# Gates of a decoder's first 128 tokens by indexed adds in a DRAM table in place of one-hot products

## The chip, the cores and the metric

One NeuronCore of a Trainium2 chip runs the whole program in one launch. The metric is device microseconds of one execution; three executions of the kernel before gave 2060.58, 2060.9 and 2061.28 us, and their median, 2060.9 us, is the time before. Its engines are called by the profile's names: PE (TensorE, matmul), PEld (its weight loads), DVE (VectorE), ACT (ScalarE), POOL (GpSimd) and SP (SyncE, which here only issues DMAs).

## What is computed

Two layers, each a mixer (gated convolution beside an mLSTM), a cross-attention on a memory, and a feed-forward part of 16,384 single-neuron experts, on 256 tokens of width 1024. The change is in the last part:

```
q  = (xb @ w_pq).reshape(tokens, 8 heads, 2, 128)
sc = einsum('thpc,hpkc->thpk', q, sub_keys)        # two score lists of 128 keys per head
sv, si = top_k(sc, 16)
cand = sv[..., 0, :, None] + sv[..., 1, None, :]   # 256 sums
fv, fi = top_k(cand, 16)
eid = row key * 128 + column key                   # of each of the 16
g   = softmax(fv)
a   = gelu(ue[eid] . xb)
out = sum over heads and k of g * a * ve[eid]
```

The kernel does not gather experts. It computes the Gelu of all 16,384 for all tokens, multiplies by a dense table of gates, gate[column key, row key, token], which is zero for what was not chosen, and multiplies with all of v_experts. What has to be made is that table: per token 8 heads x 16 weights, added at (row, column).

## The kernel before, in words

All weights pass as 680 slabs of 128 x 1024 floats (512 KB), 340 a layer, through four slots. SP loads raw[j]; ACT copies it to w_hi[j] (in rounded form); DVE subtracts, w_lo[j] = raw[j] - w_hi[j] (`lo_part`, line 848); PE takes the products hi x (hi, lo) as one matmul of 512 columns (line 1345) and lo x hi as one of 256 (line 1346), eight such chunks a slab. A slot is free again when PE is done with it, so DVE can be up to four slabs ahead of PE, and SP's loads four ahead of DVE.

In each layer the experts' first side (U) has 128 slabs, the second (V) 128. In U slab n PE makes 128 x 256 sums; ACT copies one half (`half_of`, line 721) and splits the slab n + 4 (line 725), DVE adds the other half (`add_u`, line 1113), ACT takes the Gelu (`gelu_of`, line 731), and SP stores the 128 KB of h_out in DRAM (h_park). h_out has two slots, so `half_of` waits for the store of two slabs before. In V, SP loads those back (h_in), POOL multiplies each by gate[:, n, :] (`gated`, line 524), ACT and DVE split the product, and PE multiplies it with the slab (line 1733).

While PE works through U slabs 4 to 71, DVE also makes the choice, as a written-out list of instructions. `top16` (lines 1126 to 1138) takes the 16 largest of two rows at a time, for 32 score lists and 16 candidate lists (one block of 128 tokens on the partitions after the other). Then come the decoding of the places into keys (lines 1172 to 1206, with 2 x 16 picks of 256 elements and two trees), ACT's Exp of all weights at U slab 60 (`EXP_AT`, line 753), and their normalising (lines 1211 to 1213, `decoded`). Between these, `spend(us)` adds up an assumed cost and emits `next_lo()` (one `add_u` and one `lo_part`) for each 1.56 us of it (`LO_EVERY`), so the order on DVE is fixed when the program is built. Steps that depend on the one before are joined by a semaphore (`step.join`, `step.link`).

At U slab 70 (`RET_AT`) PE waits for `decoded` and transposes the rows, columns and weights of both token blocks (line 1697, six transposes), so that tokens lie on the free axis. From slab 72 (`HOT_AT`) to 123, 64 groups of four tokens follow: DVE builds one-hots (`hot_rows`, lines 1228 to 1242, four operations of 512 elements), PE multiplies column one-hots by weighted row one-hots, 4 tokens x 2 parts a group (`gates_of`, line 1708), and ACT copies the 128 x 512 result into the gate table (`gate_out`, line 761). GROUP_AT places the groups between PE's chunks, in pairs, one pair every 13 chunks.

POOL's queue in a layer, in order: a load of memT, sums of squares (line 494), scaling of z, sums of squares of the x after the mixer; then the wait for the slab XO_AT and the load of the keys skT (line 507), the sums of squares before the queries, whose result PE needs for the norm (x_mean_square), scaling of the queries; then a wait for the last one-hot and the load of par (line 516); then the 128 multiplies of V. During U it has nothing to do.

Of the kernel before, what the change touches and what calls it, by code (L numbers as in the profile page):

```python
# [22 lines left out]
FP32 = mybir.dt.float32  # L23
# [9 lines left out]
P = 128  # L33
# [66 lines left out]
GROUPS = T // 4  # L100
HOT_AT = 72
RET_AT = 70
EXP_AT = 60
# [5 lines left out]
GROUP_AT = tuple(FIRST_PAIR + (n - n % 2) * HOT_SLABS * KB // GROUPS for n in range(GROUPS))  # L109
EARLY = RING - 1  # L110
# [39 lines left out]
def trunk(nc, x, mem, slabs, params, sub_keys, out):  # L150
    ctx = ExitStack()
    with ctx:
# [50 lines left out]
        pick_at = at("pick_at", top[0], [P, 2, T // 2, 2], FP16)  # L203
        g_parts = at("g_parts", top[0] + 2 * T * 2, [P, T // 2, PARTS, 2], FP16)
        top[0] += (2 + PARTS) * T * 2
        top[0] = (top[0] + LINE - 1) // LINE * LINE
        gated_at = top[0]
        gate = sb("gate", [P, NKEYS, T])
# [78 lines left out]

        h_park = nc.dram_tensor("h_park", (NKEYS, P, T), FP32, kind="Internal").ap()
# [48 lines left out]
        settled = sem("settled")  # L337
        act_step, dve_step, out_ready = sem("act_step"), sem("dve_step"), sem("out_ready")
# [119 lines left out]
        def _(pool):  # L458
# [11 lines left out]

            def scale(dst, count, evacs, xns):
# [25 lines left out]
            for layer in range(DEPTH):  # L497
# [7 lines left out]
                sum_chunks(layer, SUM_OUT, 0)  # L505
                pool.wait_ge(slab_done, layer * SLABS + XO_AT)
# [11 lines left out]
                settle(pool)  # L518

                def gated(g, j, h, n):  # L520
# [3 lines left out]
                    nc.gpsimd.tensor_tensor(h[:, n:n + 1, :], h[:, n:n + 1, :], gate[:, ds(g * RING + j, 1), :],  # L524
                                            ALU.mult).then_inc(gated_ready, 1)
# [16 lines left out]
        def _(act):  # L542
# [73 lines left out]
            for layer in range(DEPTH):  # L616
# [142 lines left out]
                def gate_out(n):  # L759
                    act.wait_ge(gate_mm, layer * GROUPS + n + 2)  # L760
                    nc.scalar.activation(gate[:, :, 4 * n:4 * n + 4],  # L761
                                         ps[:, 4 + n % RING, :].rearrange("p (t i) -> p i t", t=4),
                                         ACT.Copy, scale=1.0 / GATE_SCALE).then_inc(gate_copied, 1)
# [78 lines left out]
        def _(dve):  # L842
# [119 lines left out]
            for layer in range(DEPTH):  # L962
# [179 lines left out]
                for n in range(0, TB * SETS, 2):  # L1142
                    if n % SETS == 0:
                        dve.wait_ge(sc_evac, layer * TB + n // SETS + 1)
                        settle(dve)
                    src = (scores0, scores1)[n // SETS]
                    step.join()
                    top16(*[(src[:, m % SETS, :], struck[:, m - n, 0:NKEYS], top_v[:, m, :], top_u[:, m, :])
                            for m in (n, n + 1)], us=0.29)
                step.join()  # L1150
                step.mark(nc.vector.tensor_copy(top_i[:], top_u[:]))

                step.join()
                for b in range(TB):
                    tops = top_v[:, b * SETS:(b + 1) * SETS, :].rearrange("p (h s) a -> p h s a", s=2)
                    step.join()
                    first = 0
                    for a0, na, nb in CAND:
                        shape = [P, PH, na, nb]
                        step.mark(nc.vector.tensor_tensor(  # L1160
                            cand[:, :, first:first + na * nb].rearrange("p h (a b) -> p h a b", a=na),
                            tops[:, :, 0, a0:a0 + na].unsqueeze(3).to_broadcast(shape),
                            tops[:, :, 1, 0:nb].unsqueeze(2).to_broadcast(shape), ALU.add))
                        first += na * nb
                    spend(1.3)
                    for n in range(b * PH, (b + 1) * PH, 2):
# [3 lines left out]
                step.join()  # L1170

                nc.vector.tensor_tensor(g_exp[:], fin_v[:], fin_v[:, :, 0:1].to_broadcast([P, TB * PH, TOPK]),
                                        ALU.subtract).then_inc(fin_ready, 1)
                flat_i = fin_i[:].rearrange("p c k -> p (c k)")
                step.mark(nc.vector.tensor_scalar(bit_u[:], flat_i, 8, None, ALU.bitwise_and))
                step.mark(nc.vector.tensor_scalar(low_u[:], flat_i, 7, None, ALU.bitwise_and))
                step.mark(nc.vector.tensor_scalar(by16_u[:], flat_i, 4, None, ALU.logical_shift_right))
                step.mark(nc.vector.tensor_scalar(by8_u[:], flat_i, 3, None, ALU.logical_shift_right))
                step.mark(nc.vector.tensor_copy(at_f[:], flat_i))
                spend(1.6)  # L1180
                step.join()


                step.mark(nc.vector.scalar_tensor_tensor(bit_f[:], at_f[:], float(CAND[0][1] * CAND[0][2]), bit_u[:],
                                                         ALU.is_lt, ALU.mult))
                step.mark(nc.vector.scalar_tensor_tensor(b_f[:], at_f[:], float(N_CAND - CAND[2][1]), low_u[:],
                                                         ALU.is_lt, ALU.mult))
                step.mark(nc.vector.scalar_tensor_tensor(a_f[:], by8_u[:], -2.0, by16_u[:], ALU.add, ALU.max))
                step.join()
                step.mark(nc.vector.tensor_tensor(b_at[:], b_f[:], bit_f[:], ALU.add))  # L1190
                step.mark(nc.vector.scalar_tensor_tensor(a_at[:], at_f[:], float(CAND[2][0] - (N_CAND - CAND[2][1])), a_f[:],
                                                         ALU.add, ALU.max))
                spend(2.2)
                keys = top_i[:].rearrange("p (c s) a -> p c s a", s=2)
                for side, (place, found) in enumerate(((a_at, row_f), (b_at, col_f))):
                    step.join()
                    for a in range(TOPK):
                        step.mark(nc.vector.scalar_tensor_tensor(  # L1198
                            pick[:, a], place[:].rearrange("p (c k) -> p c k", k=TOPK), float(a),
                            keys[:, :, side, a].unsqueeze(2).to_broadcast([P, TB * PH, TOPK]), ALU.is_equal, ALU.mult))  # L1200
                        spend(0.45)
                    n = TOPK // 2
                    while n:
                        step.join()
                        out = found[:].rearrange("p (o c k) -> p o c k", o=1, k=TOPK) if n == 1 else pick[:, 0:n]
                        step.mark(nc.vector.tensor_tensor(out, pick[:, 0:n], pick[:, n:2 * n], ALU.add))
                        spend(0.13 * n + 0.2)
                        n //= 2
                step.join()
                dve.wait_ge(gexp_ready, layer + 1)  # L1210
                step.link(nc.vector.tensor_reduce(g_sum[:], g_exp[:], AX.X, ALU.add))
                step.link(nc.vector.reciprocal(g_sum[:], g_sum[:]))
                nc.vector.scalar_tensor_tensor(g_exp[:], g_exp[:], GATE_SCALE,
                                               g_sum[:].unsqueeze(2).to_broadcast([P, TB * PH, TOPK]),
                                               ALU.mult, ALU.mult).then_inc(decoded, 1)
# [3 lines left out]
                step.mark(nc.vector.tensor_copy(pick_at[:].rearrange("p i n e -> p (i n e)"), ps[:, 4, :]))  # L1219
                g_pairs = ps[:, 5, 0:T].rearrange("p (n e) -> p n e", e=2)  # L1220
# [111 lines left out]
        def _(pe):  # L1332
# [94 lines left out]
            for layer in range(DEPTH):  # L1427
# [267 lines left out]
                for i, src in enumerate((row_f[:], col_f[:], g_exp[:].rearrange("p c k -> p (c k)"))):  # L1695
                    for b in range(TB):
                        last = nc.tensor.transpose(ps[:, 4 + i // 2, (i % 2) * T + b * P:(i % 2) * T + (b + 1) * P],
                                                   src[:, b * P:(b + 1) * P], ident[:])
# [117 lines left out]
```

## Time and profile before

| | |
|---|---|
| median of three executions | 2060.9 us (2060.58 to 2061.28) |
| the profiled execution's own time | 2061.37 us |
| its span, first to last instruction | 2059.6 us |
| PE, PEld busy | 99%, 85% |
| DVE, ACT, POOL busy | 80%, 58%, 16% |
| granted TensorE clock, mean | 0.999 |
| DMA, mean over the span | 211 GB/s |

The profile shows one execution. Busy shares are averages over stages with different limits; the windows give them by stage. An instruction's row says when it began, how long it lasted and, in brackets, how long its engine had been idle and what ended that; instructions of one engine are pipelined, so the distance between two starts can be shorter than a duration. In layer 0 the choice runs from about 288 us, the gate groups from 493 to 665 us, and V from 678 us.

### The profile page before, as it was taken

How to read it: one execution, taken by the hardware profiler on the slowest of the kernel's cores; microseconds unless marked ns; L12 is line 12 of the kernel's file. 1: busy time of each engine (PE TensorE's matmuls, PEld its weight loads, DVE VectorE, ACT ScalarE, POOL GpSimd, SP SyncE). 2: the span in 40 equal slices, each digit the busy share in tenths (PEclk: the TensorE clock that was granted, in tenths of full speed). 3: DMA queues.
4: the chain of work that ended last, by engine and by line, in shares of the span. 5: the costliest groups of instructions: out<-in, count | busy, mean ns of one | idle time of the engine just before them, and what ended most of it. 6: DMA issues, size and time to landing. Idle time of an engine off the chain costs nothing.

```text
span 2059.6 us, 38391 instructions
## 1 busy us (share of the span) xinstructions
PE 2042.0 (99%) x11552; PEld 1756.4 (85%) x11552; DVE 1643.4 (80%) x3047; ACT 1190.0 (58%) x1901; POOL 337.0 (16%) x342
## 2 busy tenths in 40 slices
PE   8999999999999999999999999999999999999998
PEld 7888888888888888888888888888888898888886
DVE  7785869999998667767688858799999986776666
ACT  6655556667666555555565545666666665545553
POOL 3010110000000333335330102000000004333331
PEclk9999999999999999999999999999999999999999
DMA  6445456776555877777654555566665567777773
GB/s 232 148 154 175 172 193 237 236 233 216 196 199 196 265 241 241 262 241 242 211 188 135 186 170 169 195 237 236 223 215 197 200 215 255 240 241 262 242 241 124
DMA packets 174249, 435.54 MB, mean 211 GB/s; under 512 B 19504, under 2 KB 85040, under 8 KB 173136
## 3 DMA queue, kind: packets, MB, share of 16 engines
q1 hardware_dynamic: 173520, 430.06, 62.2%
q0 software_dynamic: 640, 4.32, 0.6%
q8 instruction: 53, 0.87, 0.2%
q14 instruction: 36, 0.29, 0.1%
HBM read 397.60 MB, written 36.70 MB: 211 GB/s over the span
## 4 chain that ended last, share of the span: by engine, by line
PE 93%; DVE 4%; ACT 1%; DMA 1%; issue 1%; SPq 0%; DVEq 0%; ACTq 0%
PE ps L1733 33%; PE ps L1345 32%; PE ps L1346 16%; PE ps L1708 3%; PE ps L1624 2%; PE ps L1339 2%; DVE w_lo L848 1%; DMA raw<-slabs 1%; PE ps L1755 1%; PE ps L1683 1%; PE ps L1649 1%; PE ps L1606 1%; ACT w_hi L725 0%; DMA h_park<-h_out 0%; DVE pick L1198 0%
## 5 line engine op out<-in xcount | busy, mean ns | idle before, releaser
L848 DVE TENSOR_TENSOR w_lo<-raw,w_hi 128x1024 fp32r<-128x1024 f32 x674 | 838.2, 1244 | 265.9 <-ACT w_hi L793 195.4
L1345 PE MATMUL ps<-act,w_hi 128*128 128x512 f32 x2784 | 986.0, 397 | 0.0
L1346 PE MATMUL ps<-act,w_lo 128*128 128x256 f32 x2784 | 776.4, 279 | 0.0
L1345 PEld LDWEIGHTS ps<-act,w_hi 128*128 128x128 f32 x2784 | 521.9, 187 | 115.2 <-issue 0.4
L1733 PE MATMUL ps<-w_hi,act 128*128 128x512 f32 x1936 | 596.4, 389 | 0.0
L1346 PEld LDWEIGHTS ps<-act,w_lo 128*128 128x128 f32 x2784 | 525.0, 189 | 0.3
L793 ACT ACTIVATE w_hi<-raw 128x1024 fp32r<-128x1024 f32 x248 | 263.1, 1061 | 326.8 <-PE ps L1733 326.8
L1733 PEld LDWEIGHTS ps<-w_hi,act 128*128 128x128 f32 x1936 | 363.4, 188 | 75.7
L1733 PE MATMUL ps<-w_lo,act 128*128 128x512 f32 x968 | 376.6, 389 | 0.0
L524 POOL TENSOR_TENSOR h_in<-h_in,gate 128x256 f32<-128x256 f32 x250 | 243.6, 976 | 437.5 <-DMA h_in<-h_park 437.5
L725 ACT ACTIVATE w_hi<-raw 128x1024 fp32r<-128x1024 f32 x248 | 261.1, 1053 | 0.0
L1733 PEld LDWEIGHTS ps<-w_lo,act 128*128 128x128 f32 x968 | 181.7, 188 | 37.5
L552 ACT ACTIVATE w_hi<-raw 128x1024 fp32r<-128x1024 f32 x168 | 177.1, 1054 | 47.9 <-PE ps L1346 26.6
L1264 DVE TENSOR_TENSOR act<-h_in,act 128x256 fp32r<-128x256 f32 x250 | 184.5, 738 | 4.9 <-ACT act L781 4.9
L731 ACT ACTIVATE h_out<-h_out 128x256 f32<-128x256 f32 x248 | 103.2, 416 | 124.6 <-DVE h_out L1113 122.8
L721 ACT ACTIVATE h_out<-ps 128x256 f32<-128x256 f32 x248 | 94.6, 382 | 120.5 <-PE ps L1346 106.8
L516 POOL DMA_DIRECT2D par<-params x2 | 1.2, 592 | 785.7 <-DVE hot_row L1242 785.7
L1113 DVE TENSOR_TENSOR h_out<-h_out,ps 128x256 f32<-128x256 f32 x248 | 102.1, 412 | 16.3 <-ACT h_out L721 16.0
L781 ACT ACTIVATE act<-h_in 128x256 fp32r<-128x256 f32 x250 | 100.0, 400 | 8.3 <-POOL h_in L524 8.3
L1242 DVE TENSOR_TENSOR hot_row<-row_is,g_parts 128x512 f16<-128x512 f16 x256 | 96.5, 418 | 0.0
L1345 PE MATMUL ps<-pre,w_hi 128*128 128x512 f32 x216 | 77.1, 400 | 0.0
L761 ACT ACTIVATE gate<-ps 128x512 f32<-128x512 f32 x128 | 70.4, 591 | 6.0 <-PE ps L1708 6.0
(268 smaller groups left out, 1818.3 us busy)
## 6 DMA issues: line engine op xcount, KB each, us to landing
raw<-slabs SPq DMA_DIRECT2D x680, 512.0 KB, 4.2
h_park<-h_out SPq DMA_DIRECT2D x256, 128.0 KB, 2.1
h_in<-h_park SPq DMA_DIRECT2D x250, 128.0 KB, 3.9
memT<-mem POOLq DMA_DIRECT2D x2, 1024.0 KB, 7.9
skT<-sub_keys POOLq DMA_DIRECT2D x2, 1024.0 KB, 6.3
x_park<-xT SPq DMA_DIRECT2D x2, 1024.0 KB, 6.4
xT<-x_park SPq DMA_DIRECT2D x2, 1024.0 KB, 7.3
xT<-x SPq DMA_DIRECT2D x4, 256.0 KB, 5.7
```

The costliest lines, as they stand in the source:

```text
L524: nc.gpsimd.tensor_tensor(h[:, n:n + 1, :], h[:, n:n + 1, :], gate[:, ds(g * RING + j, 1), :], ALU.mult).then_inc(gated_ready, 1)
L552: nc.scalar.activation(w_hi[:, j].rearrange("p k c -> p (k c)"), raw[:, j, :], ACT.Copy).then_inc(hi_ready, 1)
L725: nc.scalar.activation(w_hi[:, j].rearrange("p k c -> p (k c)"), raw[:, j, :], ACT.Copy).then_inc(hi_ready, 1)
L731: nc.scalar.activation(slot, slot, ACT.Gelu).then_inc(act_evac, 1)
L781: nc.scalar.activation(hi[:, j:j + 1, :], h[:, j:j + 1, :], ACT.Copy).then_inc(ga_hi_ready, 1)
L793: nc.scalar.activation(w_hi[:, j].rearrange("p k c -> p (k c)"), raw[:, j, :], ACT.Copy).then_inc(hi_ready, 1)
L848: nc.vector.tensor_tensor(w_lo[:, j].rearrange("p k c -> p (k c)"), raw[:, j, :], w_hi[:, j].rearrange("p k c -> p (k c)").bitcast(FP32), ...
L1113: nc.vector.tensor_tensor(slot, slot, ps[:, n % RING:n % RING + 1, 0:T], ALU.add).then_inc(u_sum, 1)
L1264: nc.vector.tensor_tensor(lo[:, j:j + 1, :], h[:, j:j + 1, :], hi[:, j:j + 1, :].bitcast(FP32), ALU.subtract).then_inc(ga_ready, 1)
L1345: nc.tensor.matmul(ps[:, j, :], w_hi[:, j, k, :], a[:, :, k, :], start=(k == 0), stop=False)
L1346: return nc.tensor.matmul(ps[:, j, hi * T:hi * T + T], w_lo[:, j, k, :], a[:, hi, k, :], start=False, stop=(k == KB - 1))
L1733: last = nc.tensor.matmul(ps[:, 2 * b + half, :], a[:, j, b * P:(b + 1) * P], w[:, j, 4 * half:4 * half + 4, :].rearrange("p k c -> p (k c)"),
```

## The change

The gates of tokens 0 to 127 are no longer made by one-hot products. A DRAM table g_spread of 128 x 128 x 128 floats (column key, row key, token) is zeroed by POOL during the query projections (eight stores of 1 MB, each awaited). For these tokens DVE computes an index, (column x 128 + row) x 128 + token, and the normalised weight; POOL then issues, per head, 16 indirect DMAs that add 128 weights (one per partition) at 128 indices each, and waits for a head's 16 before it goes on. When all eight heads are in, four loads of 2 MB bring the table into the first half of the gate tile, gate[:, 0]. Tokens 128 to 255 keep the one-hots, with 32 groups instead of 64, into gate[:, 1].

The choice is cut in three parts, (block 0, heads 0 and 1), (block 0, heads 2 to 7) and (block 1, all heads), each with its own top-16 steps, decoding, Exp and weights. A part's weights come after the first pair of the next part. ACT's Exps come at U slabs 12, 36 and 72; RET_AT moves from 70 to 78, HOT_AT from 72 to 80. PE transposes three matrices instead of six. The spend() figures are scaled to the parts' widths.

```diff
-GROUPS = T // 4
-HOT_AT = 72
-RET_AT = 70
-EXP_AT = 60
+GROUPS = P // 4
+HOT_AT = 80
+RET_AT = 78
+CHOICES = ((0, 0, 2), (0, 2, PH), (1, 0, PH))
+EXP_ATS = (12, 36, 72)
+ZERO_ROWS = 16
+BACK_ROWS = 32
...
-        gate = sb("gate", [P, NKEYS, T])
+        gate = sb("gate", [P, TB, NKEYS, P])
...
+        g_spread = nc.dram_tensor("g_spread", (P * NKEYS * P, 1), FP32, kind="Internal").ap()
...
 (POOL)
+            spread = g_spread.rearrange("(p n t) o -> p n (t o)", p=P, n=NKEYS)
...
                 sum_chunks(layer, SUM_OUT, 0)
+                nc.gpsimd.memset(zeros[:], 0.0).then_inc(zeros_set, 1)
+                pool.wait_ge(zeros_set, layer + 1)
+                for i in range(NKEYS // ZERO_ROWS):
+                    pool.dma_start(spread[:, i * ZERO_ROWS:(i + 1) * ZERO_ROWS, :], zeros[:]).then_inc(zeroed, 16)
+                    pool.wait_ge(zeroed, layer * (NKEYS // ZERO_ROWS * 16) + (i + 1) * 16)
                 pool.wait_ge(slab_done, layer * SLABS + XO_AT)
                 pool.dma_start(skT[:], ...)
...
+                for h in range(PH):
+                    for p in range(2):
+                        if h == CHOICES[p][1]:
+                            pool.wait_ge(place_ready, layer * 4 + 2 * p + 2)
+                    for i in range(h * TOPK, (h + 1) * TOPK):
+                        nc.gpsimd.indirect_dma_start(g_spread, bass.IndirectOffsetOnAxis(ap=place_u[:, i:i + 1], axis=0),
+                                                     g_flat[:, i:i + 1], None, compute_op=ALU.add).then_inc(scattered, 16)
+                    pool.wait_ge(scattered, (layer * PH + h + 1) * (TOPK * 16))
+                for n in range(0, NKEYS, BACK_ROWS):
+                    pool.dma_start(gate[:, 0, n:n + BACK_ROWS, :], spread[:, n:n + BACK_ROWS, :]).then_inc(spread_back, 16)
                 pool.wait_ge(hot_row_ready, (layer + 1) * GROUPS + 1)
...
+                pool.wait_ge(spread_back, (layer + 1) * (NKEYS // BACK_ROWS * 16))
...
 (ACT)
-                experts(RING, EXP_AT - RING)
-                act.wait_ge(fin_ready, layer + 1)
-                nc.scalar.activation(g_exp[:], g_exp[:], ACT.Exp).then_inc(gexp_ready, 1)
-                experts(EXP_AT, HOT_AT - RING - EXP_AT)
+                at = RING
+                for p, (b, h0, h1) in enumerate(CHOICES):
+                    exp_at = EXP_ATS[p]
+                    experts(at, exp_at - at)
+                    act.wait_ge(fin_ready, layer * len(CHOICES) + p + 1)
+                    chosen = g_exp[:, b * PH + h0:b * PH + h1, :]
+                    nc.scalar.activation(chosen, chosen, ACT.Exp).then_inc(gexp_ready, 1)
+                    at = exp_at
+                experts(at, HOT_AT - RING - at)
...
 (DVE)
+                def weights(p):
+                    b, h0, h1 = CHOICES[p]
...
+                    if b == 0:
+                        step.mark(nc.vector.scalar_tensor_tensor(place_f[:, own], col_f[:, flat], float(NKEYS), row_f[:, flat],
+                                                                 ALU.mult, ALU.add))
+                    dve.wait_ge(gexp_ready, layer * len(CHOICES) + p + 1)
+                    step.link(nc.vector.tensor_reduce(g_sum[:, cs], g_exp[:, cs], AX.X, ALU.add))
+                    step.link(nc.vector.reciprocal(g_sum[:, cs], g_sum[:, cs]))
+                    if b == 0:
+                        nc.vector.tensor_scalar(place_u[:, own], place_f[:, own], float(P), tok[:, 0:1],
+                                                ALU.mult, ALU.add).then_inc(place_ready, 1)
+                        nc.vector.tensor_tensor(g_flat[:, own]..., g_exp[:, cs], of_sum, ALU.mult).then_inc(place_ready, 1)
+                    else:
+                        nc.vector.scalar_tensor_tensor(g_exp[:, cs], g_exp[:, cs], GATE_SCALE, of_sum,
+                                                       ALU.mult, ALU.mult).then_inc(decoded, 1)
+                for p, (b, h0, h1) in enumerate(CHOICES):
+                    heads = h1 - h0
+                    wide = heads / PH
+                    for n in range(b * SETS + 2 * h0, b * SETS + 2 * h1, 2):
+                        step.join()
+                        top16(...)
+                        if p > 0 and n == b * SETS + 2 * h0:
+                            step.join()
+                            weights(p - 1)
+                            spend(0.9)
...
+                weights(len(CHOICES) - 1)
...
 (PE)
-                    for b in range(TB):
-                        last = nc.tensor.transpose(ps[:, 4 + i // 2, ...], src[:, b * P:(b + 1) * P], ident[:])
+                    last = nc.tensor.transpose(ps[:, 4, i * P:(i + 1) * P], src[:, P:2 * P], ident[:])
```

## Rows read from the trace of the kernel before

**Rows 1.** The page, part 1: busy us (share of the span) and instructions of each engine.

```profile
PE 2042.0 (99%) x11552; PEld 1756.4 (85%) x11552; DVE 1643.4 (80%) x3047; ACT 1190.0 (58%) x1901; POOL 337.0 (16%) x342
```

**Rows 2.** Windows: stretch, its us, busy us of each engine, clock, DMA share, GB/s.

```profile
140.00:235.00 95.00, 95.00 (x514) 82.46 (x514) 65.14 (x84) 49.15 (x80) 5.99 (x7) 1.00 0.49 166
...
320.00:484.00 164.00, 164.00 (x949) 144.61 (x948) 155.63 (x488) 106.52 (x180) 0.00 (x0) 1.00 0.69 231
```

**Rows 3.** Chain that ended last: start us, us, what; first and last of the gate pairs.

```profile
484.16 0.66 PE ps L1697 x6
...
504.23 0.98 PE ps L1708 x16
...
663.77 0.93 PE ps L1708 x16
```

**Rows 4.** Timeline of ACT around layer 1's Exp: start us, us, instruction, shapes.

```profile
1478.40 1.28 ACT L753 ACT_TABLE_LOAD   x1
...
1481.43 0.38 ACT L721 ACTIVATE h_out<-ps 128x256 f32<-128x256 f32 x1
1481.71 1.05 ACT L725 ACTIVATE w_hi<-raw 128x1024 fp32r<-128x1024 f32 x1
1482.78 1.28 ACT L731 ACT_TABLE_LOAD   x1
1484.07 0.42 ACT L731 ACTIVATE h_out<-h_out 128x256 f32<-128x256 f32 x1
```

**Rows 5.** DVE's waits, 440 to 492 us: us in total, times, longest.

```profile
DVE h_out L1113 <- ACT h_out L721: 1.9, 2, 1.5
DVE w_lo L848 <- ACT w_hi L725: 1.8, 4, 0.5
```

**Rows 6.** Windows of line 1345 alone (one matmul a chunk), PE and PEld busy.

```profile
310.00:470.00 160.00, 160.00 (x463) 86.25 (x462) 1.00 0.69 231
```

**Rows 7.** Timeline of DVE at the end of layer 0's choice.

```profile
480.75 1.22 DVE L848 TENSOR_TENSOR w_lo<-raw,w_hi 128x1024 fp32r<-128x1024 f32 x1
481.89 0.41 DVE L1211 TENSOR_REDUCE g_sum<-g_exp 128x16 f32<-128x256 f32 x1
482.33 0.25 DVE L1212 RECIPROCAL g_sum<-g_sum 128x16 f32<-128x16 f32 x1
482.62 0.42 DVE L1213 SCALAR_TENSOR_TENSOR g_exp<-g_exp,g_sum 128x256 f32<-128x256 f32 x1
482.96 0.41 DVE L1113 TENSOR_TENSOR h_out<-h_out,ps 128x256 f32<-128x256 f32 x1
```

**Rows 8.** Timeline of POOL, 120 to 300 us.

```profile
207.82 0.59 POOL L507 DMA_DIRECT2D skT<-sub_keys  x1 [65.58 <-PE ps L1624]
223.07 0.80 POOL L494 TENSOR_TENSOR sq_sum<-sq 128x256 f32<-128x256 f32 x1 [14.65 <-ACT sq L588]
```

**Rows 9.** DMA issues: engine, count, KB each, median us from issue to landing.

```profile
h_park<-h_out SPq DMA_DIRECT2D x256, 128.0 KB, 2.1
...
x_park<-xT SPq DMA_DIRECT2D x2, 1024.0 KB, 6.4
xT<-x_park SPq DMA_DIRECT2D x2, 1024.0 KB, 7.3
...
par<-params POOLq DMA_DIRECT2D x2, 62.0 KB, 3.1
```

**Rows 10.** POOL by line and operation: busy us, mean ns of one, idle before.

```profile
L516 POOL DMA_DIRECT2D par<-params x2 | 1.2, 592 | 785.7 <-DVE hot_row L1242 785.7
```

**Rows 11.** Timeline of POOL, 640 to 672 us.

```profile
663.11 0.59 POOL L516 DMA_DIRECT2D par<-params  x1 [392.93 <-DVE hot_row L1242]
669.54 3.42 POOL L524 TENSOR_TENSOR early_in<-early_in,gate 128x256 f32<-128x256 f32 x3 [5.84 <-DMA early_in<-h_park]
```

**Rows 12.** The page, part 5: a DVE subtract that runs beside POOL's multiplies.

```profile
L1264 DVE TENSOR_TENSOR act<-h_in,act 128x256 fp32r<-128x256 f32 x250 | 184.5, 738 | 4.9 <-ACT act L781 4.9
```

**Rows 13.** Timeline of DVE at the load of par.

```profile
662.38 1.22 DVE L848 TENSOR_TENSOR w_lo<-raw,w_hi 128x1024 fp32r<-128x1024 f32 x1
```

More of the change, by code:

```diff
@@ L760, in gate_out @@
                     act.wait_ge(gate_mm, layer * GROUPS + n + 2)
-                    nc.scalar.activation(gate[:, :, 4 * n:4 * n + 4],
+                    nc.scalar.activation(gate[:, 1, :, 4 * n:4 * n + 4],
                                          ps[:, 4 + n % RING, :].rearrange("p (t i) -> p i t", t=4),
@@ new lines, in _ @@
+                for p, (b, h0, h1) in enumerate(CHOICES):
+                    src = (scores0, scores1)[b]
+                    if h0 == 0:
+                        dve.wait_ge(sc_evac, layer * TB + b + 1)
+                        settle(dve)
+                    heads = h1 - h0
+                    wide = heads / PH
+                    for n in range(b * SETS + 2 * h0, b * SETS + 2 * h1, 2):
+                        step.join()
+                        top16(*[(src[:, m % SETS, :], struck[:, m - n, 0:NKEYS], top_v[:, m, :], top_u[:, m, :])
+                                for m in (n, n + 1)], us=0.29)
+                        if p > 0 and n == b * SETS + 2 * h0:
+                            step.join()
+                            weights(p - 1)
+                            spend(0.9)
+                    step.join()
+                    sets = slice(b * SETS + 2 * h0, b * SETS + 2 * h1)
+                    step.mark(nc.vector.tensor_copy(top_i[:, sets, :], top_u[:, sets, :]))
+                    tops = top_v[:, sets, :].rearrange("p (h s) a -> p h s a", s=2)
@@ L1158, in _ @@
                     for a0, na, nb in CAND:
-                        shape = [P, PH, na, nb]
+                        shape = [P, heads, na, nb]
                         step.mark(nc.vector.tensor_tensor(
-                            cand[:, :, first:first + na * nb].rearrange("p h (a b) -> p h a b", a=na),
+                            cand[:, h0:h1, first:first + na * nb].rearrange("p h (a b) -> p h a b", a=na),
                             tops[:, :, 0, a0:a0 + na].unsqueeze(3).to_broadcast(shape),
@@ L1164, in _ @@
                         first += na * nb
-                    spend(1.3)
-                    for n in range(b * PH, (b + 1) * PH, 2):
+                    spend(0.2 + 1.1 * wide)
+                    for n in range(b * PH + h0, b * PH + h1, 2):
                         step.join()
@@ L1193, in _ @@
-                spend(2.2)
-                keys = top_i[:].rearrange("p (c s) a -> p c s a", s=2)
-                for side, (place, found) in enumerate(((a_at, row_f), (b_at, col_f))):
-                    step.join()
[L1197 to L1203, printed above, removed]
-                        step.join()
[L1205 to L1215, printed above, removed]
+                    step.join()
@@ new lines, in _ @@
+                    cs = slice(b * PH + h0, b * PH + h1)
+                    flat = slice(cs.start * TOPK, cs.stop * TOPK)
+                    nc.vector.tensor_tensor(g_exp[:, cs], fin_v[:, cs], fin_v[:, cs, 0:1].to_broadcast([P, heads, TOPK]),
+                                            ALU.subtract).then_inc(fin_ready, 1)
+                    flat_i = fin_i[:, cs].rearrange("p c k -> p (c k)")
+                    step.mark(nc.vector.tensor_scalar(bit_u[:, flat], flat_i, 8, None, ALU.bitwise_and))
@@ new lines, in _ @@
+                    spend(0.6 + 0.8 * wide)
+                    keys = top_i[:, sets, :].rearrange("p (c s) a -> p c s a", s=2)
+                    for side, (place, found) in enumerate(((a_at, row_f), (b_at, col_f))):
+                        step.join()
+                        for a in range(TOPK):
+                            step.mark(nc.vector.scalar_tensor_tensor(
+                                pick[:, a, cs], place[:, flat].rearrange("p (c k) -> p c k", k=TOPK), float(a),
+                                keys[:, :, side, a].unsqueeze(2).to_broadcast([P, heads, TOPK]), ALU.is_equal, ALU.mult))
+                            spend(0.08 + 0.16 * wide)
+                        n = TOPK // 2
+                        while n:
+                            step.join()
+                            out = (found[:, flat].rearrange("p (o c k) -> p o c k", o=1, k=TOPK) if n == 1
+                                   else pick[:, 0:n, cs])
+                            step.mark(nc.vector.tensor_tensor(out, pick[:, 0:n, cs], pick[:, n:2 * n, cs], ALU.add))
+                            spend(0.07 * n * wide + 0.2)
+                            n //= 2
```

80 lines of the change are left out of this document (41 added, 39 removed).

## The prediction

> **What bounds the kernel.** I read the busy shares first: TensorE (PE) is busy 99% of the span [rows 1], so only PE work taken away, or PE made to wait, moves the time. The windows say where the next limit lies: while the experts are chosen (320 to 484 us of layer 0) PE is busy in all 164 us, but VectorE (DVE) is busy 155.63 of them, 8.4 us short of full [rows 2]. So PE sets the pace, and DVE is just able to keep it. PE's own prices come from the chain of waits: the six transposes behind the choice take 0.66 us, and the gate products stand in it as pairs of groups, 16 matmuls each, from 504.23 to 663.77 us, 29 equal periods of 5.50 us [rows 3]. ScalarE (ACT) has slack in the mean, but the Exp of the choice costs it three table loads, and DVE then waits [rows 4, 5].
>
> **What is removed.** A pair period holds 13 chunks of slab products (one chunk is a product against w_hi and one against w_lo). Without gates, 463 chunks take 160 us, 0.3456 us each [rows 6]; 13 take 4.49, so a pair of groups costs 5.50 - 4.49 = 1.01 us. (The chain shows 0.93 to 0.98 us for the 16 matmuls; with 0.93 the sum below falls by 2.6 us.) With 32 groups instead of 64, 16 pairs a layer go: 16 x 1.01 x 2 layers = 32.3 us. Three of six transposes go: 0.33 x 2 = 0.7 us. Together **-33 us**, all on PE, with nothing beside it. ACT's gate copies and DVE's one-hots halve too; both lay beside PE and give no time by themselves.
>
> **What DVE gets.** RET_AT moves from 70 to 78, so the choice gets 8 more slabs of 8 chunks: 22.1 us. Against it, per layer:
> - 8 more slabs to split: subtract 1.14 and an add of 256 elements 0.34 us, start to start [rows 7]: 11.8 us.
> - 117 more instructions (61 outside the top-16 steps become 178: three parts each for the copy, the candidate sums, the decoding, the 32 picks and the tree, and 13 instead of 3 for the weights). The same elements are cut smaller, so each new one costs its fixed part. 1024 elements take 1.14 and 256 take 0.34 us in a row [rows 7]: 1.04 ns an element, 0.07 fixed. 117 x 0.07 = 8.2 us, and 0.4 us for the three 128-element operations that build indices and weights.
> - 36 more joins (56 for 20): a dependent start comes 0.44 after the one before, an independent one 0.34 [rows 7]: 3.6 us.
> - two more Exps. With its table load and the next one an Exp holds ACT from 1478.40 to 1481.43, and a third load of 1.28 us follows at 1482.78 [rows 4]; DVE then waited 1.9 + 1.8 = 3.7 us [rows 5]: 7.4 us for two.
>
> That is 31.4 against 22.1: 9.3 us short. DVE had 8.4 us idle, 3.7 of it from that Exp, and part of the rest is gaps in dependent steps; I let 3.3 us absorb it and take **+6 us a layer, 12 in all**. Bounds: 0 (all absorbed, DVE may run up to four slabs ahead) and 9.3 a layer.
>
> ACT's waits for the three parts cost nothing: by the spend() sums the parts end when DVE has started 10, 35 and 69 slabs, and ACT asks after gelu_of(11), (35) and (71), which need DVE's slabs 15, 39 and 75. DVE's waits for the Exps are covered the same way, the weights being put off behind the next part's first pair. `decoded` falls when DVE has started 78 slabs and PE asks after 78; before it was 71 against 70.
>
> **Zeroing.** POOL idled 65.58 us before the key load at 207.82 [rows 8], and there the zeros now go: setting them (a few us), then eight 1 MB stores, one awaited before the next. By the nearest landings, 6.4 us for a 1 MB store and 7.3 for a load [rows 9], 51 to 58 us. Queued behind them are the key load and the sums whose first starts at 223.07 [rows 8], so up to about 9.5 us a store costs nothing. Beyond it the norm before the queries, and then PE, wait one for one.
>
> **The indexed adds.** 128 per layer, 16 a head, and POOL waits for each head to land. No row shows one. Lower bound: a plain POOL DMA of 128 partitions holds it 0.59 us [rows 10]. Upper: it waits out each one, 3.1 us, the landing of the smallest POOL DMA [rows 9]. I take **1.2 us**, twice the first row, which has the same count of partitions: an index must be fetched for each. Place in time: slab n of layer 0 starts at 484.16 - (70 - n) x 2.765 us [rows 3, 6]. Heads 0 and 1 are ready when DVE has started 17 slabs, PE some two behind, 332 us; heads 2 to 7 at 45 slabs, about 413 with the delay above. A head takes 16 x 1.2 + 3.1 = 22.3 us: the first two end at 377, the other six at 547. Reading back 8 MB at 7.3 us a megabyte, a 1 MB load beside slab and h traffic [rows 9], is 58 us: done at 605. POOL's first multiply, at 669.54 before [rows 11], moves to 669.5 - 16.5 + 6 = 659. So **54 us of cover**: the adds are free up to (659 - 413 - 58 - 18.6) / 96 = 1.76 us each.
>
> **Stores of h.** Their two slots are the tightest DMA: a store lands in 2.1 us [rows 9]. Adds and readback share the DMA engines with them, 0.69 in use during the choice [rows 2]. I take **+4 us in all**; bounds 0 and the second rival's 32.
>
> **The sum.** The profiled execution took 2061.4 us, 1.8 outside its span and 0.5 above the median of 2060.9. 2061.4 - 33 + 12 + 4 = 2044.4, or 2044 against the median. With 0 for both additions it is 2028; with 18.6 and 10, 2057: the forecast's own range.
>
> **Rivals.**
> *A, POOL is late (0.20).* From 1.76 us an add on, the gate's first half arrives after PE could start the values, and each 0.1 us more costs 9.6 us a layer. At 1.85 the gain is gone. At 2.2: 96 x 0.44 x 2 = 84 us, **2128**, slower; at the 3.1 bound heads 0 and 1 also run 24 us over, some 2350. For it: 1.76 lies between my bounds, an add needs more than a plain DMA. Against: issue in the trace is a fifth of the landing. The Trainium skill (DMA: Bandwidth & Descriptors, Anatomy of one DMA) puts about 2.0 us of fixed cost on a POOL DMA, most of it the wait for the write's receipt, not descriptor making. By that rule POOL is held far less than 2.0; were it held all of them, 96 x 0.24 x 2 = 46 us give 2090. The trace agrees with the split: 0.59 held, 3.1 to land.
>
> *B, the stores of h are late (0.14).* A slot must be free again in two slabs, 5.53 us; copy 0.38, split 1.05 and Gelu 0.42 [rows 4] leave 3.68 for the store. If the tiny adds on the same DMA engines double 2.1 to 4.2 us, each slab takes 0.26 us more, over the 61 slabs from 17 to 78 some 16 us a layer: +32, **2076**. It decides from a landing of about 4.0 us. Against it: the 1 MB key load beside slabs left PE busy in all 95 us of its stretch [rows 2].
>
> *C, POOL holds DVE up (0.06).* Beside POOL's multiply a DVE subtract of 256 elements takes 738 ns [rows 12]; an operation of that size elsewhere lasts 0.42 us [rows 7]. If an add does the same to DVE, some 100 of the 128 fall in the choice, where DVE has nothing to spare: 100 x 0.32 x 2 = 64 us, **2108**. Against it: beside the POOL DMA of 663.11 [rows 11] the subtract that began at 662.38 lasted its usual 1.22 us [rows 13]. The Trainium skill (SBUF — State Buffer, Who interferes with whom) says that a DVE instruction with two SBUF inputs contends with a POOL instruction that reads SBUF. By that rule 2108 would follow if fetching indices counts as such a read; no run here shows it.
>
> **How the numbers follow.** Forecast 0.60, A 0.20, B 0.14, C 0.06. This measurement can tell 0.2%, about 4 us, from no change. Faster: 0.58 of the forecast and 0.03 of B (landing under 4.0) make 0.61. The same: 0.02 of the forecast, 0.02 of A, 0.04 of B, 0.08. Slower: 0.18 of A, 0.07 of B, 0.06 of C, 0.31. The range runs from 2028 less a microsecond to C's 2108, and leaves out what of A lies beyond 2.1 us an add.
>
> **What would show it.** Right: 512 gate matmuls instead of 1024, pair periods of 22 chunks plus 1.01 us; POOL's add groups ending well ahead of the values' start and its first multiply waiting for early_in, not for the readback; DVE near full until `decoded`, PE with a few us of waits on the subtracts of slabs 40 to 78; ACT with three Exps a layer. Wrong: PE idle before the values (A); ACT waiting on h_park in tens of us (B); DVE's 1.22 us subtracts stretched beside POOL's issues (C); PE waiting in the norm before the queries (zeroing over 9.5 us a store). If DVE absorbed it all, PE never waits there and the time is near 2028.

## The result, and the profile after

The changed kernel took 2093.13 us in the median of 4 runs (2088.26 to 2095.04), the kernel before 2060.86: a ratio of 1.0153 [1.0135, 1.0170], **slower by 1.5%** where 2044 was forecast. The profiled execution took 2093.45 us, 0.3 above the median, with a span of 2091.7.

Part 1 of the page of the changed kernel, the answer to [rows 1]:

```profile
PE 2031.8 (97%) x11034; PEld 1737.1 (83%) x11034; DVE 1592.5 (76%) x3025; ACT 1231.4 (59%) x1901; POOL 803.4 (38%) x625
```

TensorE (PE) lost 518 matmuls, 512 of them gate products, but only 10 us of busy time, and it now stands idle 60 us (before: 18). ScalarE (ACT) gained 41 us, though it copies 64 gate groups less. The windows say where PE stands (us of the stretch, then PE, PEld, DVE, ACT and POOL busy, granted clock, DMA share, GB/s): the zeroing beside the queries, the choice of layer 0, the end of the hot stage in layer 0, and the same end in layer 1 in five pieces.

```profile
140.00:235.00 95.00, 95.00 (x518) 82.83 (x517) 65.49 (x84) 49.33 (x80) 12.10 (x16) 1.00 0.69 254
284.00:517.00 233.00, 226.24 (x1294) 196.38 (x1293) 206.97 (x713) 179.35 (x267) 134.84 (x75) 0.99 0.76 208
640.00:660.00 20.00, 14.33 (x97) 12.26 (x96) 8.63 (x18) 4.83 (x10) 2.24 (x4) 0.93 0.96 382
660.00:690.00 30.00, 25.26 (x144) 21.98 (x143) 16.19 (x24) 15.48 (x30) 3.93 (x4) 0.82 0.82 284
...
1679.00:1690.00 11.00, 11.00 (x78) 9.72 (x76) 5.42 (x12) 3.24 (x7) 1.28 (x3) 1.00 0.99 403
1690.00:1700.00 10.00, 5.20 (x30) 4.30 (x29) 1.36 (x2) 0.94 (x2) 0.00 (x0) 0.91 1.01 426
1700.00:1712.00 12.00, 3.47 (x20) 2.66 (x21) 7.57 (x15) 6.76 (x13) 0.54 (x1) 0.50 0.76 293
1712.00:1718.00 6.00, 6.00 (x28) 5.18 (x27) 1.85 (x3) 3.32 (x7) 0.00 (x0) 0.73 0.77 227
1718.00:1730.00 12.00, 12.00 (x101) 11.96 (x100) 8.30 (x9) 6.55 (x12) 3.15 (x3) 1.00 0.87 280
```

The zeroing lies where [rows 2] had PE full, and PE is still full. The choice has lost its fullness, though, and during the readback (382 and 426 GB/s) PE stops and the clock it is granted falls, to 0.50 between 1700 and 1712 us.

The chain of waits of the changed kernel (start, us, what) names what PE stood behind:

```profile
371.22 3.87 DMA h_park<-h_out
...
399.53 1.28 ACT L759
...
443.32 4.83 DMA h_park<-h_out
...
642.22 10.42 DMA h_park<-h_out
654.62 13.49 DMA h_park<-h_out
...
695.17 337.31 PE ps L1802 x1488
...
1679.00 10.22 DMA h_park<-h_out
1691.18 15.21 DMA h_park<-h_out
```

Where before a store of h landed in 2.1 us in the median [rows 9], the chain has stores of mostly 3.1 to 4.9 us in the choice and two a layer of 10 to 15 us in the readback; and it has ScalarE's table loads (the 1.28 us at 399.53). The values, the run of 1488 matmuls, start at 695.17 us; in the chain before they started at 678.35.

Two more views carry the rest. ACT's waits for the slots of h (total, times, longest; the kernel before had 12.9 us in 15 waits, 2.0 the longest):

```profile
ACT h_out L759 <- DMA h_park<-h_out: 98.8, 71, 10.4
```

And POOL's lines: the adds (busy us, mean ns of one, then idle before them), the issue of the readback, both as DMAs (count, KB each, median us from issue to landing), and for the readback's loads the shortest, median and longest landing:

```profile
L542 POOL DMA_INDIRECT g_spread<-g_flat,place_u x256 | 455.2, 1778 | 282.2 <-DVE g_flat L1202 153.2 <-issue 91.7 <-DMA g_spread<-g_flat,place_u 37.3
...
640.66 2.24 POOL L547 DMA_DIRECT2D gate<-g_spread  x4 [2.80 <-DMA g_spread<-g_flat,place_u]
...
g_spread<-zeros POOLq DMA_DIRECT2D x16, 1024.0 KB, 5.7
gate<-g_spread POOLq DMA_DIRECT2D x8, 2048.0 KB, 17.3
...
DMA to landing us min/median/max: 9.4/17.3/25.5
```

An add holds POOL 1.78 us and the next follows 0.38 us later (91.7 us in 240 gaps): 2.16 from start to start, where 1.2 was taken. The four loads of 2 MB are issued in 2.24 us, together; one lands after 17.3 us in the median and the last after about 25, so the 8 MB are in some 26 us after the first issue (640.7 to 667.1 us in layer 0), where 58 were taken.

### The profile page after: what moved, and what is told of

It is laid out like the page before. It is cut to its first block, busy times and chain, and to the rows that moved or that the text cites. A ratio compares the mean times of both kernels' runs of the same rounds, so it can differ in the third digit from the quotient of the medians.

```text
span 2091.7 us, 37604 instructions
## 1 busy us (share of the span) xinstructions
PE 2031.8 (97%) x11034; PEld 1737.1 (83%) x11034; DVE 1592.5 (76%) x3025; ACT 1231.4 (59%) x1901; POOL 803.4 (38%) x625
## 4 chain that ended last, share of the span: by engine, by line
PE 75%; DVE 11%; DMA 6%; ACT 5%; issue 2%; SPq 0%; ACTq 0%; DVEq 0%
PE ps L1802 32%; PE ps L1416 22%; PE ps L1417 11%; DMA h_park<-h_out 6%; DVE w_lo L891 4%; ACT w_hi L763 2%; PE ps L1695 2%; PE ps L1410 2%; PE ps L1777 1%; DVE h_out L1156 1%; ACT h_out L769 1%; PE ps L1824 1%; PE ps L1754 1%; PE ps L1720 1%; PE ps L1677 1%
## 5 line engine op out<-in xcount | busy, mean ns | idle before, releaser
L891 DVE TENSOR_TENSOR w_lo<-raw,w_hi 128x1024 fp32r<-128x1024 f32 x674 | 840.4, 1247 | 293.4 <-ACT w_hi L836 189.1
L1416 PE MATMUL ps<-act,w_hi 128*128 128x512 f32 x2784 | 997.3, 401 | 23.5 <-ACT h_out L769 12.3
L542 POOL DMA_INDIRECT g_spread<-g_flat,place_u x256 | 455.2, 1778 | 282.2 <-DVE g_flat L1202 153.2
L562 POOL TENSOR_TENSOR h_in<-h_in,gate 128x256 f32<-128x256 f32 x250 | 238.8, 956 | 444.5 <-DMA h_in<-h_park 444.5
L1335 DVE TENSOR_TENSOR act<-h_in,act 128x256 fp32r<-128x256 f32 x250 | 190.8, 763 | 6.2 <-ACT act L824 6.2
L511 POOL TENSOR_TENSOR sq_sum<-sq 128x256 f32<-128x256 f32 x4 | 4.5, 1137 | 184.6 <-ACT sq L626 184.6
L1417 PE MATMUL ps<-pre,w_lo 128*128 128x256 f32 x216 | 60.4, 280 | 0.0
## 6 DMA issues: line engine op xcount, KB each, us to landing
gate<-g_spread POOLq DMA_DIRECT2D x8, 2048.0 KB, 17.3
```

The lines of the kernel that those rows point to most:

```text
L542: nc.gpsimd.indirect_dma_start(g_spread, bass.IndirectOffsetOnAxis(ap=place_u[:, i:i + 1], axis=0), g_flat[:, i:i + 1], None, compute_op=A ...
L562: nc.gpsimd.tensor_tensor(of_h, of_h, gate[:, :, ds(g * RING + j, 1), :], ALU.mult).then_inc(gated_ready, 1)
L891: nc.vector.tensor_tensor(w_lo[:, j].rearrange("p k c -> p (k c)"), raw[:, j, :], w_hi[:, j].rearrange("p k c -> p (k c)").bitcast(FP32), ...
L1335: nc.vector.tensor_tensor(lo[:, j:j + 1, :], h[:, j:j + 1, :], hi[:, j:j + 1, :].bitcast(FP32), ALU.subtract).then_inc(ga_ready, 1)
L1416: nc.tensor.matmul(ps[:, j, :], w_hi[:, j, k, :], a[:, :, k, :], start=(k == 0), stop=False)
L1417: return nc.tensor.matmul(ps[:, j, hi * T:hi * T + T], w_lo[:, j, k, :], a[:, hi, k, :], start=False, stop=(k == KB - 1))
```

## The experiments

All times are medians; the kernel before stood at 2063.1, 2061.3 and 2061.5 us beside the three sets of runs (1 to 4, 5 to 8, 9 and 10), and at 2060.9 beside the change. Differences in us are of medians; across sets they can be off by these 2 us, and there the ratios decide.

| run | what differs | us | ratio to before |
|---|---|---|---|
| the change | | 2093.1 | 1.0153 [1.0135, 1.0170] |
| 1 | readback in loads of 512 KB | 2075.4 | 1.0059 [1.0042, 1.0076] |
| 2 | no readback | 2058.9 | 0.9979 [0.9969, 0.9989] |
| 3 | no readback, no adds | 2053.8 | 0.9960 [0.9947, 0.9972] |
| 4 | before, half the gate groups | 2030.6 | 0.9844 [0.9828, 0.9860] |
| 5 | a Gelu behind each Exp | 2072.0 | 1.0052 [1.0035, 1.0069] |
| 6 | four slots for stores of h | 2076.3 | 1.0063 [1.0046, 1.0080] |
| 7 | run 5, readback spread into the values | 2044.2 | 0.9919 [0.9903, 0.9936] |
| 8 | runs 6 and 7 together | 2033.1 | 0.9858 [0.9842, 0.9875] |
| 9 | runs 3 and 5 together | 2032.2 | 0.9855 [0.9838, 0.9871] |
| 10 | before, four slots | 2062.2 | 1.0000 [0.9990, 1.0009] |

### Runs 1 to 4: what each part costs

**Run 1.** The same readback in a quarter of the row length:

```diff
-BACK_ROWS = 32
+BACK_ROWS = 8
```

> Edit: the table is read back in 16 loads of 512 KB (rows of 4 KB) instead of 4 of 2 MB (rows of 16 KB). Theory 1, packet size: two stores of h landed in 10.4 and 13.5 us during the readback because each of their small packets waits for a 16 KB packet (611 ns) on its DMA engine; with 4 KB packets (159 ns) a store lands in about 4.5 us, PE does not stop and its clock does not fall, and the time drops from 2093 by about 30 us to 2063 (2055 to 2070). Rival, bytes: what delays the stores is 8 MB of extra traffic however it is cut; then the time stays at 2085 to 2095.

18 us came back, between the two theories. ACT's longest wait for a store fell from 10.4 to 5.8 us, but POOL's first multiply now waited for the readback itself, up to 26 us (in the change it waited for early_in), and the chain still has a store of 9.67 us:

```profile
ACT h_out L759 <- DMA h_park<-h_out: 86.9, 82, 5.8
...
POOL early_in L562 <- DMA gate<-g_spread: 43.9, 2, 26.0
...
654.43 9.67 DMA h_park<-h_out
```

The Trainium skill (DMA: Bandwidth & Descriptors, Queues, rings and completion order) says that a DMA engine turns from one queue to the next only after a whole packet. The fall with the shorter rows agrees with it in direction only: the chain of run 1 has stores of 5.7 to 9.7 us at the readback, in place of 10.2 to 15.2, and not theory 1's 4.5. The row length is not shown to be the cause either, as the 16 loads were also issued over 8.5 us instead of 2.2, which spreads them; no run parts the two. The same 8 MB still cost 16.5 us over run 2, in late stores and in POOL's wait for the last load; how it divides is not shown.

**Run 2.** The readback gives way to a fill with zeros on POOL:

```diff
-                    pool.dma_start(gate[:, 0, n:n + BACK_ROWS, :], spread[:, n:n + BACK_ROWS, :]).then_inc(spread_back, 16)
+                    nc.gpsimd.memset(gate[:, 0, n:n + BACK_ROWS, :], 0.0).then_inc(spread_back, 1)
```

> Edit: the table is not read back; POOL sets the first half of the gate tile to zero instead, so the experts' part of tokens 0 to 127 is left out of the output. Theory 1 and its rival alike: what the readback costs goes, 17 us a layer (10 us of idle PE and 7 of half clock): 2059 (2052 to 2064). Rival, late adds: if it is the end of the adds that PE waited for, nothing changes, 2088 to 2095.

The readback is worth 2093.1 - 2058.9 = **34 us** (36 by the ratios), the largest cost of the change.

**Run 3.** Run 2, and POOL issues no adds:

```diff
-                    for i in range(h * TOPK, (h + 1) * TOPK):
-                        nc.gpsimd.indirect_dma_start(g_spread, ...)
-                    pool.wait_ge(scattered, ...)
```

> Edit: as the run without the readback, and the 128 indexed adds a layer are left out too (the three-part choice with its indices and weights stays). Theory A, the adds delay the stores of h during the choice: about 8 us a layer below the run without the readback, near 2042. Theory B, the three-part choice alone overloads DVE and ACT: within 4 us of the run without the readback, near 2057. Theory C, POOL's descriptor work holds DVE's port: like A, but with DVE's subtracts shorter than beside adds.

The 256 adds are worth **5 us**, nearer to theory B than to A. What is left is the choice in three parts beside 32 gate groups, and it still is 23 us above run 4.

**Run 4.** The kernel before with 32 groups instead of 64; POOL zeroes the other half of the gate:

```diff
-GROUPS = T // 4
+GROUPS = P // 4
...
+                nc.gpsimd.memset(gate[:, :, P:T], 0.0).then_inc(rest_zeroed, 1)
```

> Edit: the kernel before with 32 groups instead of 64 and nothing else of the change (one-part choice, six transposes, no table); the gates of tokens 128 to 255 are set to zero by POOL, so their experts' part is left out. It prices the PE term of the prediction alone: 32 us below 2061, 2029 (2026 to 2033). Rival: if the gate stage was held by DVE or ACT, or gets nothing back, 2045 to 2061.

2063.1 - 2030.6 = **32.6 us**: the gain on PE, against 33 forecast. Laid end to end, the change is 2030.6 + 23 (choice in three parts) + 5 (adds) + 34 (readback) = 2093. That it adds up is no proof, each term being the difference of two neighbouring runs; the check is that runs 5, 7 and 9 below take the parts away in another order.

### Runs 5 and 9: the 23 us of the choice

The lines of ACT tell of them: the table loads before (first three; count, busy us, mean ns, idle before)

```profile
L721 ACT ACT_TABLE_LOAD x6 | 7.7, 1283 | 0.1
L731 ACT ACT_TABLE_LOAD x6 | 7.7, 1283 | 0.1
L753 ACT ACT_TABLE_LOAD x2 | 2.6, 1283 | 0.0
```

and after, at the same three lines (copy of the sum, Gelu, Exp):

```profile
L759 ACT ACT_TABLE_LOAD x34 | 43.6, 1283 | 0.6
L769 ACT ACT_TABLE_LOAD x34 | 43.6, 1283 | 0.6
L795 ACT ACT_TABLE_LOAD x6 | 7.7, 1283 | 0.1
```

60 more loads are 77 us of ACT. The timeline of ACT at the first Exp of the changed kernel shows where they stand:

```profile
325.58 1.28 ACT L795 ACT_TABLE_LOAD   x1
326.88 0.23 ACT L795 ACTIVATE g_exp<-g_exp 128x32 f32<-128x32 f32 x1
327.12 1.28 ACT L759 ACT_TABLE_LOAD   x1
328.42 0.38 ACT L759 ACTIVATE h_out<-ps 128x256 f32<-128x256 f32 x1
...
329.77 1.28 ACT L769 ACT_TABLE_LOAD   x1
...
338.84 1.28 ACT L759 ACT_TABLE_LOAD   x1
340.13 0.39 ACT L759 ACTIVATE h_out<-ps 128x256 f32<-128x256 f32 x1
...
341.49 1.28 ACT L769 ACT_TABLE_LOAD   x1
```

The first slab behind the Exp loads two tables (327.12, 329.77), and so does the first slab of the *next* pass of four (338.84, 341.49), though no Exp lies between; the other three slabs of a pass load none. The load is an instruction of the program's loop: a loop that is entered with the Exp's table in place carries the loads in its body and runs them in every pass. The count fits: with Exps at slabs 12, 36 and 72 the loops behind them make 6, 9 and 1 passes a layer, and with the first pass of the stage that is 17, or 34 in two layers. The Trainium skill (ScalarE activation tables: per-element evaluation and per-set limits, Table sets in the compiler and the runtime) says that the loads are placed per block of code; these rows agree.

**Run 5.** One element of Gelu behind each Exp, so that every loop is entered with Gelu's table:

```diff
                     nc.scalar.activation(chosen, chosen, ACT.Exp).then_inc(gexp_ready, 1)
+                    nc.scalar.activation(warm[:], eps[:], ACT.Gelu)
```

> Edit: the changed kernel, with one Gelu of a single column issued right after each of the three Exps, before the loop that follows. Theory T: with an Exp ahead of a loop, every pass of the loop loads ACT's two tables again (34 loads each of the copy's and the Gelu's line, 6 each before; 56 more of 1.28 us are 72 us of ACT time), and this is most of the 23 us that the three-part choice costs without adds; with the Gelu's table in place at the loop's start the loads go, and the time falls by 15 to 20 us, from 2093 to 2075 (2070 to 2080). Rival D: the cost is DVE's, in 117 more instructions and 36 more joins; then 2088 to 2095.

21 us came back, and the loads are gone from the loops:

```profile
L795 ACT ACT_TABLE_LOAD x6 | 7.7, 1283 | 0.1
L796 ACT ACT_TABLE_LOAD x6 | 7.7, 1283 | 0.1
...
L759 ACT ACT_TABLE_LOAD x2 | 2.6, 1283 | 0.0
L769 ACT ACT_TABLE_LOAD x2 | 2.6, 1283 | 0.0
```

**Run 9.** The same edit on run 3, to see whether anything of the choice's cost is VectorE's (DVE):

> The changed kernel with neither adds nor readback (POOL writes zeros into the gates of tokens 0 to 127, whose experts so drop out), and with a one-element Gelu behind each Exp, so that the passes of ScalarE's loop don't reload their tables. Theory: the +23 us that the choice in three parts still cost without adds and readback are mostly the table loads, and go as the 21 us of the Gelu run did: 2033 (2030 to 2037), 0 to 6 above the kernel with half the gate groups, with two table loads at each Gelu line instead of 34. Rival 1 (the prediction's term): DVE's instructions cost 12 of it whatever ScalarE does: 2042. Rival 2: the loads only mattered because the adds and the readback had made the stores of h late: 2050 or more.

The ratio fell from 0.9960 to 0.9855, by 21.6 us, to 0.0011 (2 us) above run 4. The windows of both choices of run 9 have PE full, with DVE 17 and 19 us short of full:

```profile
284.00:505.00 221.00, 221.00 (x1292) 193.73 (x1291) 204.02 (x715) 143.77 (x244) 13.94 (x4) 1.00 0.68 221
1287.00:1512.00 225.00, 225.00 (x1293) 195.83 (x1292) 205.57 (x716) 144.69 (x246) 13.94 (x4) 1.00 0.68 221
```

So DVE took in the smaller pieces, the joins and the 8 slabs for some 2 us in all (by the intervals of the two ratios at most 7), and the table loads were nearly all of the 23.

### Runs 6, 7, 8 and 10: the stores of h

**Run 6.** The changed kernel with four slots for h instead of two, each still stored two slabs after the copy, so that a late store holds up nothing at once:

```diff
-H_SLOTS = 2
+H_SLOTS = 4
+STORE_LAG = 2
...
+        h_more = sb("h_out_more", [P, 2, T])
```

> Edit: the changed kernel with four slots for h_out instead of two. Theory: stores of h that land late are what stops ACT, in the choice (adds) and in the readback; two more slots give a store two more slabs, 5.5 us, so the two stores of 10 and 13 us a layer cost half, and the short waits of the choice vanish: 2093 to about 2070 (2063 to 2080). Rival: ACT and DVE are late by their own work and would be late without waiting for a store: 2088 to 2095.

ACT no longer waits for a store of h at all, and 17 us came back, but not the 34 of the readback. What is late next are the slabs; ACT's waits of this run now have

```profile
ACT w_hi L768 <- DMA raw<-slabs: 49.3, 22, 11.1
```

So with all 8 MB in the DMA engines at once the wait moved, from the stores to the slabs; more slots did not end it.

**Run 7.** Run 5 with the readback in 16 blocks of 8 rows, four on their way and a further one issued as POOL turns to the next block that is in, so that 11 of the 16 fall into the values' stage:

```diff
+                for b in range(BACK_AHEAD):
+                    back(b)
...
+                    pool.wait_ge(spread_back[b % BACK_AHEAD], ...)
+                    if b + BACK_AHEAD < NKEYS // BACK_ROWS:
+                        back(b + BACK_AHEAD)
```

> Edit: as the run with the Gelu after each Exp, and the table is read back in 16 blocks of 8 rows (512 KB), four ahead: four before the values, the others during them. Theory: the readback's remaining cost is 8 MB at one time beside the tightest stores; spread over the values it costs nearly nothing (the values have 247 GB/s of traffic and waits to spare): the run with 32 groups alone, 2031, plus 5 of the adds and about 5 of the three Exps, 2041 (2036 to 2048). Rival: the values, with PE full and DMA 0.75 in use, pay for 6 MB more: 2050 or above.

Another 28 us came back against run 5. **Run 8** is this with the four slots of run 6:

> Edit: as the run before this one, and four slots for h_out. Theory: what is left of the adds' cost is late stores, and goes: 2036 (2032 to 2042), faster than both kernels by 1.2% over the kernel before. Rival: the adds cost POOL or DVE, not stores: as the run before this one.

2033.1 us, 11 less than run 7, 1.4% faster than before and 1 us above run 9, which has neither adds nor readback. PE is full in the choice and nearly so at the stage's end, though POOL works 133 us beside it:

```profile
284.00:506.00 222.00, 222.00 (x1300) 196.42 (x1299) 205.93 (x716) 143.90 (x246) 133.00 (x71) 1.00 0.81 222
640.00:665.00 25.00, 24.57 (x178) 22.49 (x177) 12.29 (x18) 13.29 (x26) 7.15 (x11) 1.00 0.97 322
```

**Run 10** is the control: the slots of run 6 in the kernel before.

> The kernel before with four slots for the stores of h instead of two, stored two slabs later as ever: a control for what the slots gain without the change. Theory: its stores land in 2.1 us and PE waits for nothing, so the 12.9 us that ScalarE waits for them cost no time: 2061 (2057 to 2063), and the gain of the slots in the changed kernel is repair of what the change did to the stores. Rival: the stores cost the kernel before too, up to those 12.9 us: 2048 to 2056, and part of the combined version's gain has nothing to do with the change.

Nothing changed, so the slots repair what the change does to the stores and win nothing by themselves.

## Why the prediction was wrong

**-33 us on PE: right.** Run 4 measured 32.6. The price of a pair of groups, 1.01 us from [rows 3, 6], held.

**Zeroing at nothing: right.** The eight stores of a layer landed in 5.7 us each in the median, under the 9.5 that were free, and PE stayed full from 140 to 235 us.

**"+6 us a layer, 12 in all" for DVE: wrong in kind.** The choice cost 23 us, beyond even the bound of 9.3 a layer (18.6 in all), and DVE's share of it is some 2 (run 9). The step that failed is "two more Exps". It counted three table loads to an Exp from [rows 4] and charged DVE 3.7 us for each, as an event that passes. It did not ask how often the two loads behind an Exp are run. The trace before could have told: six loads at the copy's line and six at the Gelu's, for two Exps, are three a layer at each, one for the stage's first pass and one for *each* of the two passes of the loop behind the Exp. With the first Exp moved from slab 60 to slab 12, 17 passes a layer reload. The 58 loads that run 5 took away are 74 us of ACT and were worth 21; the rest of their time lay beside PE's work.

**"+4 us" for the stores of h: the mechanism was right, the source and the size were not.** The second rival let the tiny adds double the landing of a store. They did not: from 284 to 505 us a store landed in 2.7 us in the median with adds (run 7) and in 2.2 without (run 9), both under the deciding point of 4.0, and stores of 3 to 5 us stand in the chain of run 3 too, which has no adds. The adds were worth 5 us (run 2 against run 3), and by what way is not shown: the slots of run 8 took back 11 of the 12 us by which run 7 stands above run 9, which points at the stores, but run 7 holds adds and readback together. The step that failed is the readback's: named beside the adds, it was costed as a transfer with cover, 8 MB at 7.3 us a megabyte, and so as free, and it was worth 34. The wrong number there is 58 us: the DMA engines took all 8 MB at once and were done in 26 us, moving 382 GB/s in all from 640 to 660 us, and for that time the stores of h queued behind it. A row of the kernel before pointed the other way: the key load beside slabs left PE full [rows 2]; but that is 1 MB, not 8.

**A term that was missing: the clock.** The rows from 1690 on show it: PE is busy 5.20 of 10 us, then 3.47 of 12, and the granted clock goes from 1.00 through 0.91 to 0.50, the lower of its two levels, and is back at 1.00 by 1718. Matmuls that take 0.39 and 0.28 us at full clock take 0.63 and 0.41 behind the wait, early in the stretch whose mean is 0.73:

```profile
1694.69 0.39 PE L1416 MATMUL ps<-act,w_hi 128*128 128x512 f32 x1
1694.92 0.28 PE L1417 MATMUL ps<-act,w_lo 128*128 128x256 f32 x1
1703.19 0.79 PE L1416 MATMUL ps<-act,w_hi 128*128 128x512 f32 x1 [8.00 <-DVE w_lo L891]
...
1710.55 1.01 PE L1777 MATMUL ps<-hot_row,hot_col 128*128 128x128 f16 x8 [4.91 <-DVE hot_row L1313]
...
1714.03 0.63 PE L1416 MATMUL ps<-act,w_hi 128*128 128x512 f32 x1
1714.45 0.41 PE L1417 MATMUL ps<-act,w_lo 128*128 128x256 f32 x1
```

So a wait of PE is paid twice, once as idle time and once as slow matmuls behind it. The mean clock was 0.991 with the change, 0.997 in run 2 and 0.999 in run 8. 0.006 of 2091.7 us, some 12 us, is an upper bound for the clock's share of the readback's 34, as PE stood idle in part of it.

**Rival A, POOL late: its price came true, its effect stayed hidden.** The adds of heads 2 to 7 began at 414.9 us (413 forecast), but took 2.16 us each, above the 1.76 at which A was to decide, and the last was in at 640.7 us instead of 547. A's sum held the 58 us of readback. With 26 the limit is (659 - 413 - 26 - 18.6) / 96 = 2.10 us, and the adds stand just above it. Still POOL did not wait for the readback, which was in at 667: its first multiply came at 685 and not at 659, for PE and the stores of h were late by then, and it waited for early_in:

```profile
685.26 3.39 POOL L562 TENSOR_TENSOR early_in<-early_in,gate 128x256 f32<-128x256 f32 x3 [9.18 <-DMA early_in<-h_park]
```

That is luck: two wrong numbers, 1.2 and 58, nearly cancelled, and the other delays hid the rest. Run 1 shows A's wait, and in run 8 the first multiply came at 660.5 us with the adds in at 646.2, so that 26 us of readback would have been late.

The Trainium skill's rule that was weighed there (DMA: Bandwidth & Descriptors, Anatomy of one DMA), by which making descriptors is the small part of a POOL DMA's fixed cost, does not fit an indexed add: 1.78 us held, and 2.80 from the last add's end until its landing is seen.

**Rival C, POOL holds DVE up: not seen.** The subtract of 1024 elements had a mean of 1247 ns over 674, before 1244. Most of these lie away from the adds, so here are those from 415 to 505 us alone, where POOL issues adds, after and before:

```profile
L891 DVE TENSOR_TENSOR w_lo<-raw,w_hi 128x1024 fp32r<-128x1024 f32 x31 | 38.0, 1226 | 5.2 <-ACT w_hi L763 4.7
...
L848 DVE TENSOR_TENSOR w_lo<-raw,w_hi 128x1024 fp32r<-128x1024 f32 x31 | 37.9, 1221 | 3.1 <-ACT w_hi L725 2.9
```

In run 3, without adds, it was 1222 there.

The Trainium skill's rule on DVE and POOL reads (SBUF — State Buffer, Who interferes with whom) thus does not reach to the fetching of indices here.

ACT's wait for the first part cost nothing, as forecast: the Exp's load at 325.58 follows without an idle time. The range held the result, the sign was wrong: the choice, at 23 us, was booked at 12, and adds and readback, at 39 together, at 4.

## What to carry to other kernels

A function that needs another activation table is priced by the passes of the loop behind it, not by its own calls; one throwaway call of the loop's function ahead of each loop took 58 loads and 21 us away. A transfer "with cover" still fills the DMA engines: ask which short transfer with few buffers shares them, and hand out a long one in pieces, paced by whoever uses it. Here the two, with two more slots, turned 1.5% slower into 1.4% faster.

## What was not expected of the hardware

- An indexed add of 128 elements of 4 bytes holds POOL 1.78 us in the mean, three times the 0.59 of a plain POOL DMA of 128 partitions [rows 10], though it moves 512 bytes.
- 256 such adds beside a nearly full DVE and the slabs cost only 5 us (run 2 against run 3, without readback), and DVE's subtracts beside them were not longer (1226 ns, without adds 1222).
- A 128 KB store behind 8 MB of loads from another engine's queue took 10 to 15 us, five to seven times its usual 2.1.
- While PE stood idle from 1695.2 to 1703.2 us its granted clock fell to 1.2 GHz (0.50 from 1700 to 1712), and it was at 2.4 GHz again from 1718 on, when PE had been busy without a gap since 1710.6.
